# Half of each token row is gathered, the other half is brought to the experts by products with the slot matrix

## The chip, the cores and the metric

The kernel runs on one core of one Trainium2 chip. The metric is the device time of one execution in microseconds. All data is 32-bit floating point. The core has a matrix engine (TensorE, "PE" in the profile, its weight loads "PEld"), a vector engine (DVE), a scalar engine (ACT), GpSimd (POOL), a queue engine for transfers (SyncE, "SP") and 16 DMA engines that all transfers share. PE reads two operands from the on-chip memory (a stationary one, loaded first, and a moving one) and writes into eight banks of accumulators, from which ACT and DVE copy results out.

## What is computed

The reference is one step of a hybrid encoder layer for 384 tokens (256 of a prompt, 128 of eight samples) with 1024 features. The change is in its last part, the mixture of experts:

```
def _moe(h, p):
    scores = jax.nn.sigmoid((h @ p['router_w']).astype(jnp.float32))
    ...
    gates = jnp.einsum('blk,blke->ble', wsel, one_hot(eidx, N_EXPERTS))
    act = silu(einsum('ld,edf->lef', hs, we_gate)) * einsum('ld,edf->lef', hs, we_up)
    y = einsum('lef,efd->ld', act * gs[..., None], we_down)
    return y + (jax.nn.silu(h @ p['ws_gate']) * (h @ p['ws_up'])) @ p['ws_down']
```

The line left out is the group-limited choice of 8 of 64 experts for each token. Each expert has gate and up weights of 1024 x 256 and down weights of 256 x 1024, so 3 MB per expert. 384 tokens with 8 experts each make 3072 rows for the experts, 48 per expert on average.

## The kernel before, in words

Before the experts, the layer's projections, the two recurrent branches, the merge and the first normalisation run once over all tokens. Then the shared expert runs, and each token's input row (`h2_tok`, three tiles of 128 tokens x 1024 in token order) is stored to a DRAM table `h_rows` (L707, from ACT's queue).

The routed experts are done in 33 **tasks**. A task n below 32 is a pair of experts, 64 slots each, which fill the 128 columns; task 32 takes up to four overflow tiles of 32 slots. For a task:

- DVE's `spread(n)` makes the **slot matrix** `onehot`: for each of the three token tiles a 128 x 128 matrix of zeros and ones that says which token sits in which slot (L978).
- PE's `find(n)` (12 small matmuls, L2074) multiplies it with the token numbers, DVE's `ids(n)` writes the row number and the gate of each slot.
- POOL's `gather(n)` (L463) fetches the rows of 4 KB from `h_rows` with an indirect DMA, three tasks ahead, into one of three buffers `xt`.
- PE's `turn_in(n)` (L2063) turns the gathered 128 x 1024 tile by eight 128 x 128 transposes into banks 0 and 1. ACT's and DVE's `turned(n)` copy the two banks to `hgT`.
- PE multiplies `hgT` with the gate and up weights (L2108, 32 instructions; the two experts' columns run beside each other), ACT and DVE make the gated activation, PE turns it (L2115), `down(n)` multiplies it with the down weights (L2089, 16 instructions), ACT and DVE copy the result to `obuf`, and POOL's `scatter(n)` (L472) writes the rows of 4 KB to a DRAM table `y_rows`.

A 32-bit matmul is two instructions in the profile, a 32-bit transpose one. PE's order in its loop over n is written by hand: `turn_in(n + 1)`, the wait for the gate and up weights of task n, the gate and up matmuls of n, `down(n - 1)`, the transposes of the activation of n, `find(n + 3)`.

SP loads the weights (L528). There are four slots, two tasks' worth. SP waits until the gate and up matmuls of task n-2 are done and issues the four transfers for task n, then waits until `down(n-2)` is done and issues the two down transfers for task n. The wait on `down` holds back what follows it in the queue, so that at each end of a `down` six transfers of 1 MB are issued together: the down weights of one task and the gate and up weights of the next. After the last task the eight parts of each token are read back from `y_rows` and added.

`more(...)` holds the same steps for inputs with more than four overflow tiles. In this profile the gather of the tasks (L463) ran 33 times and the one in `more` not at all.

Of the kernel before, what the change touches and what calls it, by code (L numbers as in the profile page):

```python
# [4 lines left out]
F32 = mybir.dt.float32  # L5
# [53 lines left out]
def hybrid_kernel(nc, x_prompt, x_sample, c_prompt, c_sample, state_gdn_conv, state_gdn,  # L59
# [6 lines left out]
    with ctx:  # L66
# [91 lines left out]
        h_rows = nc.dram_tensor("h_rows", [T, D], F32).ap()  # L158
# [53 lines left out]
        h2_tok = [flat(zs, D), flat(gate, D), flat(lnx, D)]  # L212
        xt = flat(hT, 3 * D).rearrange("p (a n) -> p a n", a=3)
# [5 lines left out]
        onehot = flat(qkv, 2 * TILES * P, 4096).rearrange("p (a t c) -> p a t c", a=2, t=TILES)  # L219
        count = flat(lvl, NE)  # L220
# [139 lines left out]
        def _(pool):  # L360
# [90 lines left out]
            pool.wait_ge(S("h_out"), 32 + 16)  # L451
# [6 lines left out]
            def gather(n):  # L458
                pool.wait_ge(S("r_ids"), n + 1)
                if n >= 3:  # L460
                    pool.wait_ge(S("r_turn"), n - 2)
                mark()
                pool.indirect_dma_start(xt[:, n % 3, :], None, h_rows,  # L463
                                        bass.IndirectOffsetOnAxis(slot_ids[:, n % IDS, 0:1], 0),
                                        bounds_check=T - 1, oob_is_err=False
                                        ).then_inc(S(f"r_xg{n % 3}"), 16)
# [20 lines left out]
            def more(n_task):  # L487
                def gather(i, u):
                    pool.wait_ge(S("r_ids"), i * ROUND + u + 1 + past("ids"))
                    if not (isinstance(i, int) and i * ROUND + u < 2):  # L490
                        pool.wait_ge(S("r_turn"), i * ROUND + u - 1 + past("turn"))
                    mark()
                    pool.indirect_dma_start(xt[:, u % 2, :], None, h_rows,
                                            bass.IndirectOffsetOnAxis(slot_ids[:, u % ROUND, 0:1], 0),
                                            bounds_check=T - 1, oob_is_err=False
                                            ).then_inc(S(f"r_xg{u % 2}"), 16)
# [206 lines left out]
        def _(act):  # L703
# [188 lines left out]
            for t in range(3):  # L892
                load(h_rows[tok(t), :], h2_tok[t], "h_out")
# [28 lines left out]
            act.wait_ge(S("h_out"), 48)  # L922
# [50 lines left out]
        def _(dve):  # L973
# [445 lines left out]
            def spread(n):  # L1419

                hot = onehot[:, n % 2]
# [116 lines left out]
        def _(pe):  # L1538
# [518 lines left out]
            def turn_in(n):  # L2057
# [4 lines left out]
                for k in range(KC):  # L2062
                    last = tr(bank[k // 4][:, tok(k % 4)], xt[:, n % 3, tok(k)], ident[:, :])  # L2063
                sig(last, "r_turn")

            def find(n):
# [4 lines left out]
                for j, (cols, e) in enumerate(tiles_of(n)):  # L2071
                    for t in range(TILES):
                        rows = slot_rows[:, t, e, :] if n < N_PAIR else o_rows[:, t, j, :]
                        last = mm(bank[6][cols, 0:3], onehot[:, n % 2, t, cols], rows,  # L2074
# [48 lines left out]
            def more(n_task):  # L2123
                def turn_in(i, u):
                    pe.wait_ge(S(f"r_xg{u % 2}"), i * 48 + 16 * (u // 2 + 1) + past(f"xg{u % 2}"))
# [3 lines left out]
                    for k in range(KC):  # L2129
                        last = tr(bank[k // 4][:, tok(k % 4)], xt[:, u % 2, tok(k)], ident[:, :])  # L2130
# [101 lines left out]
```

## Time and profile before

| | us |
|---|---|
| median of 3 runs (1621.63 to 1632.64) | 1628.92 |
| the profiled execution, its own time | 1629.57 |
| its span, first to last instruction | 1627.8 |

| engine | busy us | share of the span |
|---|---|---|
| PE | 1298.6 | 80% |
| PEld | 755.5 | 46% |
| DVE | 525.2 | 32% |
| ACT | 239.8 | 15% |
| POOL | 161.2 | 10% |

A line of the page gives the line number of the kernel, the engine, the operation, the names written and read, and how often. In the chain of waits each piece has its start, its length and what it was; "issue" there is time in which the engine waited for nothing that the profile shows (a wait for several transfers is one such). "x32" counts instructions.

### The profile page before, as it was taken

The numbers are of one execution on the slowest core, as the hardware profiler recorded it, in microseconds if no ns is written. First come the engines' busy times: TensorE is split into PE (matmuls) and PEld (weight loads), VectorE is DVE, ScalarE is ACT, GpSimd is POOL, SyncE is SP. The second block draws the span as 40 slices with busy tenths as digits, with TensorE's granted clock in tenths as the row PEclk, the third lists the DMA queues.
The fourth block names the chain that finished last, engine by engine and source line by source line (L and its number), as shares of the span: only waits on it lengthen the run. The fifth ranks groups of instructions, "written<-read, shape, count | busy, mean of one in ns | idle before, by whom it ended". The sixth has DMA issues, their size and how long they took to land.

```text
span 1627.8 us, 15451 instructions
## 1 busy us (share of the span) xinstructions
PE 1298.6 (80%) x6250; PEld 755.5 (46%) x6250; DVE 525.2 (32%) x1085; ACT 239.8 (15%) x450; POOL 161.2 (10%) x196
## 2 busy tenths in 40 slices
PE   3789999687756998899799787878878878887446
PEld 1445555486634975796444543333333333333112
DVE  0432567445483233423325521311111111111007
ACT  2021441310010121121100211110110110110000
POOL 5000000030001400320000001010010010011000
PEclk8898899787877898999989789989888898989768
DMA  9365410300104001000550539999999999999655
GB/s 317 119 230 210 155 52 1 82 2 1 52 8 122 1 27 52 27 1 1 211 180 35 237 111 368 420 400 407 412 410 398 408 408 394 405 389 396 265 220 193
DMA packets 96504, 330.63 MB, mean 203 GB/s; under 512 B 20046, under 2 KB 37026, under 8 KB 69547
## 3 DMA queue, kind: packets, MB, share of 16 engines
q1 hardware_dynamic: 84230, 301.60, 48.0%
q0 software_dynamic: 9504, 25.18, 4.0%
q10 hardware_dynamic: 2692, 2.79, 0.6%
q8 instruction: 52, 0.85, 0.2%
q14 instruction: 26, 0.21, 0.0%
HBM read 314.75 MB, written 24.22 MB: 208 GB/s over the span
## 4 chain that ended last, share of the span: by engine, by line
PE 70%; DMA 10%; DVE 8%; issue 7%; SPq 3%; ACT 2%; POOL 0%; ACTq 0%; POOLq 0%; DVEq 0%
PE bank L2108 15%; PE bank L1610 9%; PE bank L2089 6%; DMA ring<-in_we_up_dram 6%; PE bank L1733 5%; PE bank L1794 3%; PE bank L1983 3%; PE bank L1951 3%; PE bank L1807 3%; PE bank L1804 2%; PE bank L2202 2%; SPq L528 2%; DVE inv L978 2%; DVE ring L978 2%; PE bank L2063 2%
## 5 line engine op out<-in xcount | busy, mean ns | idle before, releaser
L2108 PE MATMUL bank<-ring,rwp 128*64 128x512 f32 (+1 forms) x816 | 280.9, 693 | 123.8 <-issue 123.8
L2108 PEld LDWEIGHTS bank<-ring,rwp 128*64 128x64 f32 (+1 forms) x816 | 87.8, 157 | 289.2 <-issue 289.2
L1610 PE MATMUL bank<-hT,ring 128*128 128x384 f32 x416 | 145.4, 514 | 7.7 <-DVE hT L978 5.6
L2108 PE MATMUL bank<-MT,rwp 128*64 128x512 f32 (+1 forms) x272 | 144.7, 694 | 0.0
L987 DVE SCALAR_TENSOR_TENSOR seq_cols<-seq_cols,slot_gate,bank 128x256 f32<-128x256 f32 x33 | 22.1, 671 | 371.6 <-ACT seq_cols L710 371.6
L2089 PE MATMUL bank<-inv,rwp 128*64 128x512 f32 (+1 forms) x408 | 121.9, 615 | 8.8 <-DMA inv<-in_we_down_dram 8.8
L1610 PEld LDWEIGHTS bank<-hT,ring 128*128 128x128 f32 x416 | 83.3, 202 | 67.3 <-issue 9.8
L463 POOL DMA_INDIRECT hT<-h_rows,slot_ids x33 | 33.6, 1018 | 698.3 <-PE bank L2063 449.0
L1733 PE MATMUL bank<-hT,ring 128*128 128x384 f32 x256 | 89.6, 510 | 10.3 <-DMA ring<-in_w_in_dram 10.3
L710 ACT ACTIVATE seq_cols<-bank 128x256 f32<-128x256 f32 x36 | 13.8, 383 | 400.5 <-PE bank L2108 385.4
L1733 PEld LDWEIGHTS bank<-hT,ring 128*128 128x128 f32 x256 | 50.5, 201 | 44.2 <-DMA ring<-in_w_in_dram 10.4
L710 ACT ACTIVATE rwp<-bank 128x512 f32<-128x512 f32 (+1 forms) x101 | 43.5, 445 | 162.6 <-PE bank L1610 96.2
L978 DVE TENSOR_TENSOR inv<-inv,bank 128x256 f32<-128x256 f32 (+1 forms) x86 | 33.8, 428 | 96.2 <-PE bank L1807 90.5
L2089 PE MATMUL bank<-qkv,rwp 128*64 128x512 f32 (+1 forms) x136 | 64.0, 615 | 0.0
L2089 PEld LDWEIGHTS bank<-inv,rwp 128*64 128x64 f32 (+1 forms) x408 | 39.7, 139 | 47.0 <-issue 47.0
L1794 PE MATMUL bank<-inv 128*128 128x128 f32 x360 | 50.5, 301 | 6.2 <-POOL inv L446 6.2
L446 POOL TENSOR_TENSOR inv<-NT,lvl 128x512 f32<-128x512 f32 x18 | 22.8, 1267 | 327.7 <-DVE aT L978 280.3
L710 ACT ACTIVATE inv<-bank 128x512 f32<-128x512 f32 (+3 forms) x53 | 29.8, 571 | 147.4 <-PE bank L1794 129.6
L1794 PEld LDWEIGHTS bank<-inv 128*128 128x128 f32 x360 | 46.9, 211 | 8.1 <-POOL inv L446 8.1
L1807 PE MATMUL bank<-inv 128*128 128x64 f32 x360 | 49.0, 284 | 0.0
L446 POOL TENSOR_TENSOR inv<-MT,lvl 128x512 f32<-128x512 f32 x36 | 45.1, 1268 | 20.9 <-DVE MT L978 16.7
L1807 PEld LDWEIGHTS bank<-inv 128*128 128x128 f32 x360 | 45.9, 202 | 0.0
(362 smaller groups left out, 1799.1 us busy)
## 6 DMA issues: line engine op xcount, KB each, us to landing
ring<-in_we_gate_dram SPq DMA_DIRECT2D x51, 1024.0 KB, 13.4
ring<-in_we_up_dram SPq DMA_DIRECT2D x51, 1024.0 KB, 16.6
inv<-in_we_down_dram SPq DMA_DIRECT2D x51, 1024.0 KB, 10.9
ring<-in_w_ada_dram SPq DMA_DIRECT2D x12, 2048.0 KB, 14.2
MT<-in_we_gate_dram SPq DMA_DIRECT2D x17, 1024.0 KB, 16.7
MT<-in_we_up_dram SPq DMA_DIRECT2D x17, 1024.0 KB, 19.7
qkv<-in_we_down_dram SPq DMA_DIRECT2D x17, 1024.0 KB, 8.4
ring<-in_w_in_dram SPq DMA_DIRECT2D x7, 2048.0 KB, 9.1
```

The lines of the kernel that those rows point to most:

```text
L446: st.do(pool.tensor_tensor(NL[:, g].rearrange("p (h i) -> p h i", h=4), src, lvl[:, l, :].unsqueeze(1).broadcast_to([P, 4, P]), ALU.mult), ...
L463: pool.indirect_dma_start(xt[:, n % 3, :], None, h_rows, bass.IndirectOffsetOnAxis(slot_ids[:, n % IDS, 0:1], 0), bounds_check=T - 1, oob_ ...
L710: st.do(act.activation(out, in_, func, **kw), name, hold)
L978: st.do(V.tensor_tensor(out, a, b, op), name, hold)
L1610: last = mm(bank[4 + n % 4][:, 0:T], ring[:, u, k, tok(c)], hT[:, k, :], start=(k == 0), stop=(k == KC - 1))
L1733: last = mm(bank[bk][:, 0:T], mg_w[i % 3][:, k, tok(b % 2)], hT[:, k, :], start=(k == 0), stop=(k == KC - 1))
L1794: last = mm(bank[g][:, tok(h)], NL[:, g][:, tok(h)], X[:, g][:, tok(h)], start=True, stop=True)
L1807: last = mm(bank[g][:, 64 * h:64 * h + 64], T1[:, g][:, tok(h)], level_half(XT[:, g][:, tok(h)], l, 1), start=True, stop=True)
L1951: last = mm(bank[bk][:, 0:T], pab[w][:, k, tok(c)], yT[:, w, k, :], start=(k == 0), stop=(k == 3))
L1983: last = mm(bank[[4, 5, 6, 7, 0, 1][2 * t + i]][:, :], merged[:, k, tok(t)], w_o_sb[i][:, k, :], start=(k == 0), stop=(k == KC - 1))
L2089: last = mm(bank[4 + j][cols, :], actT[:, n % 2, tok(k)][:, cols], wd_slot[d_slot(e)][:, k, 512 * j:512 * j + 512], start=(k == 0), stop=( ...
L2108: last = mm(gu[cols, :], hgT[:, n % 2, k, cols], gate_up(gu_slot[w_slot(e)], k), start=(k == 0), stop=(k == KC - 1))
```

## The change

Every token row is split into two halves of 512. `h_rows` becomes two tables, each with one half, written by six stores and not three. The gather of a task fetches only the first half of each row (2 KB). The second half of the three `h2_tok` tiles stays on chip, and `turn_in` makes the turned second half by products: for each of four blocks of 128 features, the three token tiles' blocks as stationary operands times the three parts of the slot matrix, summed in bank 1. So `turn_in` has four transposes and twelve 128 x 128 x 128 products where it had eight transposes. As the slot matrix is now read later, it has three buffers (`hots`), the third in the place of `modT`. The path `more` gathers both halves with two DMAs.

```diff
--- before.py
+++ after.py
@@ -155,7 +155,7 @@
         over_e = ctx.enter_context(nc.sbuf_tensor("over_e", [P, N_OVER + 1], I32))
         tok_id = sb("tok_id", [P, TILES, 2])
 
-        h_rows = nc.dram_tensor("h_rows", [T, D], F32).ap()
+        h_rows = [nc.dram_tensor(f"h_rows{i}", [T, 512], F32).ap() for i in range(2)]
         y_rows = nc.dram_tensor("y_rows", [T * N_ACT, D], F32).ap()
 
 
@@ -209,14 +209,16 @@
         gu_slot = [flat(ring, 4096, 4096 * i) for i in range(3)] + [flat(MT, 4096)]
         wd_slot = [flat(t, 2048, off).rearrange("p (k n) -> p k n", k=2)
                    for t, off in ((inv, 0), (inv, 2048), (inv, 4096), (qkv, 0))]
-        h2_tok = [flat(zs, D), flat(gate, D), flat(lnx, D)]
-        xt = flat(hT, 3 * D).rearrange("p (a n) -> p a n", a=3)
+        h2_tok = [flat(zs, D, 512), flat(gate, D, 512), flat(lnx, D)]
+        xt = flat(hT, 3 * 512).rearrange("p (a n) -> p a n", a=3)
+        more_xt = flat(hT, 2 * D).rearrange("p (a n) -> p a n", a=2)
         hgT = flat(rwp, 2 * D, 2 * D).rearrange("p (a k c) -> p a k c", a=2, k=KC)
         obuf = [flat(zs, D), flat(gate, D)]
         sil = flat(seq_cols, 2 * DE).rearrange("p (a n) -> p a n", a=2)
         act_t = flat(seq_cols, 2 * DE, 2 * DE).rearrange("p (a n) -> p a n", a=2)
         actT = flat(rwp, 2 * DE, 4672).rearrange("p (a n) -> p a n", a=2)
         onehot = flat(qkv, 2 * TILES * P, 4096).rearrange("p (a t c) -> p a t c", a=2, t=TILES)
+        hots = [onehot[:, 0], onehot[:, 1], flat(modT, TILES * P).rearrange("p (t c) -> p t c", t=TILES)]
         count = flat(lvl, NE)
         n_over = flat(lvl, NE, NE)
         n_cum = flat(lvl, NE, 2 * NE)
@@ -448,7 +450,7 @@
                                                  ALU.mult), "inv_nl", hold=False)
 
 
-            pool.wait_ge(S("h_out"), 32 + 16)
+            pool.wait_ge(S("h_out"), 96)
             pool.wait_ge(S("sgu_mm"), 3)
 
             def mark():
@@ -460,7 +462,7 @@
                 if n >= 3:
                     pool.wait_ge(S("r_turn"), n - 2)
                 mark()
-                pool.indirect_dma_start(xt[:, n % 3, :], None, h_rows,
+                pool.indirect_dma_start(xt[:, n % 3, :], None, h_rows[0],
                                         bass.IndirectOffsetOnAxis(slot_ids[:, n % IDS, 0:1], 0),
                                         bounds_check=T - 1, oob_is_err=False
                                         ).then_inc(S(f"r_xg{n % 3}"), 16)
@@ -490,10 +492,11 @@
                     if not (isinstance(i, int) and i * ROUND + u < 2):
                         pool.wait_ge(S("r_turn"), i * ROUND + u - 1 + past("turn"))
                     mark()
-                    pool.indirect_dma_start(xt[:, u % 2, :], None, h_rows,
-                                            bass.IndirectOffsetOnAxis(slot_ids[:, u % ROUND, 0:1], 0),
-                                            bounds_check=T - 1, oob_is_err=False
-                                            ).then_inc(S(f"r_xg{u % 2}"), 16)
+                    for j in range(2):
+                        pool.indirect_dma_start(more_xt[:, u % 2, 512 * j:512 * j + 512], None, h_rows[j],
+                                                bass.IndirectOffsetOnAxis(slot_ids[:, u % ROUND, 0:1], 0),
+                                                bounds_check=T - 1, oob_is_err=False
+                                                ).then_inc(S(f"r_xg{u % 2}"), 16)
 
                 def scatter(i, u):
                     pool.wait_ge(S("r_oA"), i * ROUND + u + 1 + past("oA"))
@@ -890,7 +893,8 @@
                   bank[i][:, :].rearrange("p (m k) -> p m k", k=KC), ACT.Copy, "h2_tok", hold=False)
             act.wait_ge(S("h2_tok"), 6)
             for t in range(3):
-                load(h_rows[tok(t), :], h2_tok[t], "h_out")
+                for j in range(2):
+                    load(h_rows[j][tok(t), :], h2_tok[t][:, 512 * j:512 * j + 512], "h_out")
 
             for j in range(3):
                 act.wait_ge(S("sgu_mm"), j + 1)
@@ -919,7 +923,7 @@
                     act.wait_ge(S(f"r_sc{n % 2}"), 16 * (n // 2))
                 f(obuf[n % 2][:, 0:512], bank[4][:, :], ACT.Copy, "r_oA", hold=False)
 
-            act.wait_ge(S("h_out"), 48)
+            act.wait_ge(S("h_out"), 96)
             turned(0)
             for n in range(N_TASK):
                 if n + 1 < N_TASK:
@@ -1418,7 +1422,7 @@
 
             def spread(n):
 
-                hot = onehot[:, n % 2]
+                hot = hots[n % 3]
                 if n < N_PAIR:
                     tt(hot.rearrange("p t (a c) -> p t a c", a=2),
                        count_up[:, 0:HALF].unsqueeze(1).unsqueeze(1).broadcast_to([P, TILES, 2, HALF]),
@@ -2059,8 +2063,12 @@
                 if n:
                     pe.wait_ge(S("r_hgA"), n)
                     pe.wait_ge(S("r_hgD"), n)
-                for k in range(KC):
-                    last = tr(bank[k // 4][:, tok(k % 4)], xt[:, n % 3, tok(k)], ident[:, :])
+                for k in range(4):
+                    tr(bank[0][:, tok(k)], xt[:, n % 3, tok(k)], ident[:, :])
+                for k in range(4):
+                    for t in range(TILES):
+                        last = mm(bank[1][:, tok(k)], h2_tok[t][:, 512:D][:, tok(k)], hots[n % 3][:, t, :],
+                                  start=(t == 0), stop=(t == TILES - 1))
                 sig(last, "r_turn")
 
             def find(n):
@@ -2071,7 +2079,7 @@
                 for j, (cols, e) in enumerate(tiles_of(n)):
                     for t in range(TILES):
                         rows = slot_rows[:, t, e, :] if n < N_PAIR else o_rows[:, t, j, :]
-                        last = mm(bank[6][cols, 0:3], onehot[:, n % 2, t, cols], rows,
+                        last = mm(bank[6][cols, 0:3], hots[n % 3][:, t, cols], rows,
                                   start=(t == 0), stop=(t == TILES - 1))
                 sig(last, "r_ids_mm")
 
@@ -2122,12 +2130,12 @@
 
             def more(n_task):
                 def turn_in(i, u):
-                    pe.wait_ge(S(f"r_xg{u % 2}"), i * 48 + 16 * (u // 2 + 1) + past(f"xg{u % 2}"))
+                    pe.wait_ge(S(f"r_xg{u % 2}"), i * 96 + 32 * (u // 2 + 1) + past(f"xg{u % 2}"))
                     if not (isinstance(i, int) and i * ROUND + u < 1):
                         pe.wait_ge(S("r_hgA"), i * ROUND + u + past("hgA"))
                         pe.wait_ge(S("r_hgD"), i * ROUND + u + past("hgD"))
                     for k in range(KC):
-                        last = tr(bank[k // 4][:, tok(k % 4)], xt[:, u % 2, tok(k)], ident[:, :])
+                        last = tr(bank[k // 4][:, tok(k % 4)], more_xt[:, u % 2, tok(k)], ident[:, :])
                     last.then_inc(S("r_turn"), 1)
 
                 def find(i, u):
```

## Rows read from the trace of the kernel before

**Rows 1.** Page, span in 40 slices: PE clock in tenths, DMA engines' busy tenths.
```profile
PEclk8898899787877898999989789989888898989768
DMA  9365410300104001000550539999999999999655
```

**Rows 2.** Windows view, 985 to 1530 us: busy us, clock, DMA share, GB/s.
```profile
985.00:1530.00 545.00, 425.11 (x2128) 176.47 (x2124) 89.27 (x209) 56.80 (x123) 60.68 (x60) 0.88 0.99 403
```

**Rows 3.** DMA view, 985 to 1530 us: queue packets, MB, share of 16 engines; issues.
```profile
q1 hardware_dynamic: 26932, 196.13, 88.0%
q0 software_dynamic: 8761, 23.28, 11.0%
hT<-h_rows,slot_ids POOLq DMA_INDIRECT x29, 9.1
y_rows<-zs,slot_ids POOLq DMA_INDIRECT x16, 11.0
y_rows<-gate,slot_ids POOLq DMA_INDIRECT x15, 11.4
```

**Rows 4.** Chain of waits, one task of the stretch: start us, us, what.
```profile
1290.09 8.78 PE bank L2108 x32
1298.87 3.43 PE bank L2089 x16
1302.31 0.37 PE bank L2115 x2
1302.67 0.58 PE bank L2074 x12
1303.26 1.02 PE bank L2063 x8
1304.28 3.41 issue
1307.69 8.79 PE bank L2108 x32
```

**Rows 5.** Waits of PE, 985 to 1530 us: in total, times, longest us.
```profile
PE bank L2108 <- issue: 102.0, 29, 7.1
```

**Rows 6.** DMA view, 1096 to 1098 us, when only weights move.
```profile
DMA packets 106, 0.84 MB, mean 418 GB/s; under 512 B 4, under 2 KB 4, under 8 KB 4
```

**Rows 7.** DMA view, 60 to 100 us: loads whose rows are 2 KB.
```profile
q1 hardware_dynamic: 3106, 6.27, 43.4%
```

**Rows 8.** Timelines: one 32-bit product group L1794 at low clock, and later in the chain.
```profile
342.78 5.99 PE L1794 MATMUL bank<-inv 128*128 128x128 f32 x24 [1.30 <-POOL inv L446]
682.36 2.73 PE bank L1794 x24
```

**Rows 9.** Chain of waits, head of the expert stage.
```profile
959.73 4.48 DMA hT<-h_rows,slot_ids
964.25 1.98 PE bank L2063 x8
967.09 1.94 PE bank L2063 x8
969.03 7.71 PE bank L2108 x32
979.94 7.02 PE bank L2108 x32
```

**Rows 10.** Windows view at low clock: head of the stage, and inside one task.
```profile
964.00:967.00 3.00, 1.97 (x8) 1.57 (x8) 0.69 (x1) 0.60 (x1) 0.00 (x0) 0.50 0.71 262
1308.00:1312.00 4.00, 4.00 (x13) 1.39 (x11) 0.00 (x0) 0.00 (x0) 0.00 (x0) 0.57 1.03 394
```

**Rows 11.** Chain of waits, the last scatter, to its landing.
```profile
1563.25 2.97 DMA y_rows<-zs,slot_ids
```

**Rows 12.** Timeline of ACT's queue and the transpose that next needs ACT.
```profile
923.87 0.80 ACTq L707 DMA_DIRECT2D h_rows<-lnx  x1
933.66 0.14 PEld L2019 LDWEIGHTS bank<-ident,seq_cols 128*128 128x128 f32 x1 [0.24 <-issue]
```

## The prediction

> **What bounds the kernel now.** I read the slices of the page first [rows 1]. From about 980 to 1530 us the DMA engines stand at 9 or more, and the clock of PE sits between 8 and 9. That is the stage of the routed experts, the only one that the change touches. The windows view of 985 to 1530 us says it in one line [rows 2]: DMA share 0.99 at 403 GB/s, PE busy 425 of 545 us. The DMA view of the same stretch splits the engines' time [rows 3]: 88.0% for the queue with the weights (196.13 MB) and 11.0% for POOL's queue, which carries the rows of gathers and scatters (23.28 MB).
>
> The chain of waits shows one task [rows 4]. PE works 8.78 (gate and up), 3.43 (down), 0.37, 0.58 (find) and 1.02 us (`turn_in`), in all 14.18 us, and then stands 3.41 us. The next gate and up matmuls begin 17.60 us after the last ones. What PE waits for there is the last of the six weight transfers, which were issued at the end of an earlier `down`. The waits view gives the sum over the stretch: 102.0 us in 29 waits, 3.52 us each [rows 5]. So a task takes as long as its bytes need, and PE has 3.5 us to spare. The reader should also see that PE pays for this wait: the clock after it is at 0.57, so partly at the lower level of 1.2 GHz [rows 10], and a gate and up group takes 8.78 us where it took 7.02 at the full 2.4 GHz [rows 4, 9].
>
> **Part 1, the gather moves half.** In the stretch lie 29 gathers and 16 + 15 scatters [rows 3]. Both move the same rows of 4 KB, so the gathers' part is 29/60 of 23.28 MB, 11.25 MB, and 5.63 MB of that go. The price of a megabyte can be had in three ways. By the mean rate of 403 GB/s it is 2.48 us, and 5.63 MB are 14.0 us. By the queue's own share, 11.0% of 545 us for 23.28 MB, it is 2.58 us; but what is left moves in rows of 2 KB. Loads with such rows took 43.4% of 40 us for 6.27 MB, 2.77 us each MB [rows 7]. Then the gathers go from 11.25 x 2.58 = 29.0 to 5.63 x 2.77 = 15.6 us, a saving of 13.4. The upper end comes from what is left when weights alone move: 418 GB/s [rows 6] makes 469.2 us for 196.13 MB, the other 75.8 us of the stretch are 3.26 us for each MB of rows, and the saving would be 18.3. I take 14.0, which is nearest to the queue's own share, and keep 13.4 and 18.3. Per task it is 14.0/29 = 0.48 us, so 17.12 and not 17.60 us.
>
> **Part 2, the products.** `turn_in` loses four of eight transposes (0.51 of 1.02 us [rows 4]) and gains twelve products of 128 x 128 x 128, 24 instructions. The same form stands in the trace as a group of 24 at line 1794: 2.73 us at full clock, 5.99 us in a stretch at the low one [rows 8]. These are the two ends. In the stretch I take 2.73: `turn_in` then lasts 3.24 us, 2.22 more. PE's path is 14.18 + 2.22 = 16.40 us, under 17.12 by 0.72, even if gate and up stay at 8.78. With PE almost without a gap I expect the clock to stay up, gate and up at 7.02, and the path at 14.64. So the products cost nothing here; what hides them is the wait for weights. Without that cover they would cost 2.22 x 29 = 64 us.
>
> The weights' issue does not move away: SP issues at the end of a `down`, which comes 12.2 us or less after the weights of its task landed, so the transfers of the next task still stand in the queue for about 5 us. The engines do not run dry.
>
> **Part 3, the head of the stage.** Before the weights queue up there is nothing to hide behind. From the first gather on, the chain goes through `turn_in(0)`, `turn_in(1)`, gate and up (0), `turn_in(2)`, gate and up (1) and `down(0)` [rows 9]; only at the end of that does SP issue the first full batch, and from there on the DMA engines are the bound. A delay here passes to the end. The clock is at 0.50 from 964 to 967 us [rows 10]. Step by step:
> - The gather of half rows lands sooner. It took 4.48 us; the last scatter, with few rows, took 2.97 [rows 9, 11]. Between -1.5 and 0; I take -0.4, as most of the time is not the bytes'.
> - `turn_in(0)`, 1.98 us at low clock, becomes four transposes (0.99) and 24 instructions in 2.73 to 5.99. I take half of them at either clock: 5.36, so +3.4 (+1.7 to +5.0).
> - `turn_in(1)`, 1.94, becomes 3.24 at full clock: +1.3 (to +5.0, were it at low clock).
> - Gate and up (0) took 7.71 with its begin at low clock; at full clock it is 7.02 [rows 9]: -0.7 (or 0).
> - `turn_in(2)`: +2.2.
>
> Sum +5.8, from +3.0 to +12.2.
>
> From 964 to 967 us eight transposes kept PE busy 1.97 of 3.00 us, and the clock stayed at the low level [rows 10]. The Trainium skill, in "TensorE: Matmul & The Clock Gate", Part 4 (PE-mode transpose), says that a transpose doesn't count as a busy PE for the clock. By that rule the products, unlike the transposes, bring the clock up within the head, and the sum would be near the 5.8 above. If two thirds of busy time were simply too little, the head would stay at the low clock and the sum would be 12.2. This row agrees with the rule but doesn't prove it.
>
> **Edits at nothing.** ACT issues six stores and not three, at up to 0.80 us each [rows 12]; ACT's next result is wanted by the transposes that start at 933.66, some 9 us later, so up to 2.4 us are covered (2.4 if not). The stores land long before the first gather at 959.73 [rows 9], so POOL's and ACT's higher wait counts cost nothing. A gather stays one issue on POOL. It waits for `turn_in` of three tasks before, which is done a whole task before the `find` that it also needs, so a longer `turn_in` doesn't hold it, nor the scatter queued behind it. The copies of `turned` start up to 2.2 us later; behind them on ACT and DVE stand the activation of the task and `spread`, which are wanted only when gate and up end, some 8 us on. The third slot-matrix buffer adds no wait. The two-DMA gather of `more` doesn't run here.
>
> **Sum.** -14.0 + 5.8 = -8.2 us. The profiled execution took 1629.57 us, 0.65 above the median of 1628.92 and 1.77 above its span; against it the forecast is 1621.4, against the median 1620.7, so 1621. With the ends of the parts it runs from -18.3 + 3.0 = -15.3 to -13.4 + 12.2 = -1.2, 1613.6 to 1627.7.
>
> **Rivals.**
> - *The bytes buy no time.* If an engine pays for a row and not for its bytes, the 29 gathers cost what they did and only the head is left: +5.8, 1634.7 (1632 to 1641). Against it: 2 KB rows in a full stretch moved at 2.77 us per MB, close to the 2.58 of 4 KB rows [rows 3, 7]; for it: none of those is an indirect transfer. The Trainium skill, in "DMA: Bandwidth & Descriptors", Rules for kernel authors, advises to coalesce many small transfers into one large, which speaks for this rival; no row here shows an indirect transfer of 2 KB rows.
> - *PE becomes the bound, and the kernel slower.* The place is `turn_in` between a `down` and the next gate and up. The path without `turn_in` is 13.16 us with gate and up at 8.78, so it decides from a `turn_in` of 17.12 - 13.16 = 3.96 us (5.72 with gate and up at 7.02). With `turn_in` at the low clock, 0.99 + 5.99 = 6.98, the task takes 20.14 us, 2.54 more than now, 74 us over 29 tasks and with the head 1628.92 + 74 + 5.8 = 1709. With half of it low (5.36) it takes 18.52, 0.92 more, and 1661. For it: the margin of 0.72 us is small. Against it: the row of 682 us ran 24 such instructions in 2.73, and the low clock came after idle time that would then be gone.
> - *Rows cost more than their bytes, and the head is almost free.* The ends -18.3 and +3.0 together, or a little beyond: 1613 down to 1609. For it: the rate falls from 418 to 403 GB/s when rows mix in [rows 2, 6]. Against it: the queue's own share gives 2.58 us per MB, not 3.26.
>
> **How the numbers follow.** I give the forecast 0.68, no gain from the bytes 0.13, PE as the bound 0.11, the larger gain 0.08. The range reaches from the larger gain to the first rival, 1612 to 1637, and leaves out PE as the bound and the far ends of the others. A measurement of this kernel can tell about 1%, 16 us. Faster by more than that needs the larger gain beyond its ends: 0.09. Slower needs PE as the bound: 0.12. Within 1% the rest, 0.79.
>
> **What would show it.** In the profile after, POOL's queue should carry near 17.7 MB in the stretch, the DMA share should stay near 0.99 and the step from one gate and up to the next be near 17.1 us; the wait before it should shrink from 3.5 to between 0.7 and 2.5 us, and the clock there rise. The 24 product instructions should take near 2.73 us. The end of `down(0)`, now at 979.94 + 7.02 + 3.43 = 990.4 us [rows 4, 9], should come near 996. I am wrong if the DMA share falls below 0.95 or the wait before gate and up vanishes (PE is the bound), or if the step stays at 17.6 with half the bytes gathered.

## The result and the profile after

The changed kernel took 1609.61 us (median of 4 runs, 1607.46 to 1613.73), the kernel before 1630.78 in the same comparison: ratio 0.9884 [0.9841, 0.9928]. A second comparison on another chip gave 0.9893 [0.9868, 0.9919]. That is 17 to 19 us less, where 8.2 were forecast. The profiled execution took 1609.27 us, with a span of 1607.5.

The page after: the slices, in tenths as in [rows 1], and the line of POOL's queue (packets, MB, share). The clock of PE in the expert stage goes from 8 and 9 to 9 throughout.

```profile
PEclk7898899787877798899999799999999999999778
DMA  9365410300104001000532635999999999999655
...
q0 software_dynamic: 7392, 18.89, 3.1%
```

The windows view, with the columns of [rows 2, 10]: first the stage, which now ends near 1520, then 400 us of its middle, then two pieces of the head.

```profile
985.00:1520.00 535.00, 465.26 (x2774) 244.26 (x2774) 89.13 (x209) 56.80 (x123) 61.09 (x60) 0.96 0.98 402
1060.00:1460.00 400.00, 359.76 (x2139) 191.25 (x2138) 64.92 (x141) 43.56 (x94) 48.95 (x48) 0.98 1.00 411
964.00:967.00 3.00, 2.99 (x20) 2.80 (x19) 0.00 (x0) 0.00 (x0) 0.00 (x0) 0.74 0.03 14
967.00:970.00 3.00, 2.13 (x19) 2.17 (x20) 0.69 (x1) 0.60 (x1) 0.00 (x0) 1.00 0.00 0
```

DMA share and rate of the stage are about those of before, 0.98 and 402 GB/s for 0.99 and 403. What is new is PE: 465 of 535 us busy and a clock of 0.96, where it was 425 of 545 and 0.88. The DMA view of the same window answers to [rows 3].

```profile
q1 hardware_dynamic: 27061, 197.04, 89.3%
q0 software_dynamic: 6864, 17.75, 8.5%
hT<-h_rows,slot_ids POOLq DMA_INDIRECT x29, 7.2
```

POOL's queue carries 17.75 MB and not 23.28, as the change intends. The chain of waits, first through the head, then through one task, answers to [rows 9, 4]; L2070 are the products.

```profile
958.36 3.57 DMA hT<-h_rows,slot_ids
...
961.98 1.11 PE bank L2067 x4
963.09 3.92 PE bank L2070 x24
...
967.87 0.63 PE bank L2067 x4
968.50 2.68 PE bank L2070 x24
971.18 7.04 PE bank L2116 x32
...
980.39 0.59 PE bank L2067 x4
980.98 2.68 PE bank L2070 x24
983.66 7.02 PE bank L2116 x32
990.68 3.43 PE bank L2097 x16
...
1031.31 7.09 PE bank L2116 x32
1038.39 3.43 PE bank L2097 x16
1041.83 0.37 PE bank L2123 x2
1042.19 0.58 PE bank L2082 x12
1042.78 0.59 PE bank L2067 x4
1043.37 2.68 PE bank L2070 x24
1046.05 1.53 issue
1047.58 7.09 PE bank L2116 x32
```

A task takes 16.27 us here (1031.31 to 1047.58): gate and up 7.09 and not 8.78, and 1.53 us of waiting. The waits view of PE, 985 to 1515 us, says the same of the stretch, where [rows 5] had 102.0 us.

```profile
PE bank L2116 <- issue: 48.2, 28, 3.3
```

So the bytes, the products, the clock and the wait came as forecast, and still the kernel gained twice as much: the step from one gate and up to the next is 16.8 us on average over 24 tasks, where 17.1 were forecast. I split the stage at one point, the end of `down(0)`, from which on the DMA engines set the time. From the first gather to there the chain takes 30.7 us before (959.73 to 990.4) and 35.8 after: the head lost 5.1 us, near the forecast. From there to the begin of the last gate and up group, called the **stretch** below, it is 543.5 us before and 521.7 after: 21.9 us less, where 14.0 were forecast. The question is where the other 8 us are from.

### The profile page after: what moved, and what is told of

Same layout as the page of the kernel before. It is cut to its first block, busy times and chain, and to the rows that moved or that the text cites. A ratio compares the mean times of both kernels' runs of the same rounds, so it can differ in the third digit from the quotient of the medians.

```text
span 1607.5 us, 16774 instructions
## 1 busy us (share of the span) xinstructions
PE 1336.0 (83%) x6910; PEld 828.0 (52%) x6910; DVE 524.9 (33%) x1085; ACT 239.8 (15%) x450; POOL 161.7 (10%) x196
## 3 DMA queue, kind: packets, MB, share of 16 engines
q1 hardware_dynamic: 84230, 301.60, 48.2%
q0 software_dynamic: 7392, 18.89, 3.1%
## 4 chain that ended last, share of the span: by engine, by line
PE 78%; DVE 8%; DMA 5%; issue 4%; SPq 2%; ACT 2%; POOL 0%; ACTq 0%; POOLq 0%; DVEq 0%
PE bank L2116 15%; PE bank L1614 9%; PE bank L2097 7%; PE bank L2070 6%; PE bank L1737 5%; PE bank L1798 3%; PE bank L1987 3%; PE bank L1955 3%; PE bank L1811 3%; PE bank L1808 2%; DVE inv L982 2%; PE bank L2210 2%; DVE ring L982 2%; SPq L531 2%; DMA ring<-in_w_in_dram 1%
## 5 line engine op out<-in xcount | busy, mean ns | idle before, releaser
L2116 PE MATMUL bank<-ring,rwp 128*64 128x512 f32 (+1 forms) x816 | 244.9, 618 | 69.7 <-issue 69.7
L2116 PEld LDWEIGHTS bank<-ring,rwp 128*64 128x64 f32 (+1 forms) x816 | 80.5, 140 | 203.4 <-issue 202.9
L2116 PE MATMUL bank<-MT,rwp 128*64 128x512 f32 (+1 forms) x272 | 128.5, 628 | 0.0
L994 DVE COPY rwp<-bank 128x512 f32<-128x512 f32 (+1 forms) x34 | 23.2, 682 | 101.6 <-PE bank L2070 101.0
L1798 PEld LDWEIGHTS bank<-inv 128*128 128x128 f32 x360 | 46.9, 211 | 8.1 <-POOL inv L448 8.1
L448 POOL TENSOR_TENSOR inv<-MT,lvl 128x512 f32<-128x512 f32 x36 | 45.2, 1267 | 20.9 <-DVE MT L982 16.7
## 6 DMA issues: line engine op xcount, KB each, us to landing
ring<-in_w_ada_dram SPq DMA_DIRECT2D x12, 2048.0 KB, 14.3
```

Of the source, the lines that this page charges most:

```text
L448: st.do(pool.tensor_tensor(NL[:, g].rearrange("p (h i) -> p h i", h=4), src, lvl[:, l, :].unsqueeze(1).broadcast_to([P, 4, P]), ALU.mult), ...
L1798: last = mm(bank[g][:, tok(h)], NL[:, g][:, tok(h)], X[:, g][:, tok(h)], start=True, stop=True)
L2116: last = mm(gu[cols, :], hgT[:, n % 2, k, cols], gate_up(gu_slot[w_slot(e)], k), start=(k == 0), stop=(k == KC - 1))
```

## The experiments

Times are ratios to the kernel before on the same chip, with 95% intervals; us are the ratio less 1, times 1629. Executions of the kernel before lie up to 16 us apart on one chip, so a single time decides nothing. The table has every run; "order" is an edit of SP's queue that comes with the third set. The stretch is read from one profiled execution of each kernel, so a difference of a few us between two stretches is not secured; the changed kernel, profiled twice, gave 521.7 and 522.9. The profiled execution was the slowest of its kernel for the half gather alone (3.7 us over the median), no gather (6.1) and the late issue (6.9).

| kernel | ratio | us | stretch us |
|---|---|---|---|
| before | 1 | 0 | 543.5 |
| changed kernel | 0.9884 [0.9841, 0.9928] | -18.9 | 521.7 |
| half gather alone | 0.9927 [0.9902, 0.9953] | -11.9 | 531.6 |
| products alone | 1.0024 [0.9996, 1.0052] | +3.9 | 539.5 |
| changed kernel, again | 0.9893 [0.9868, 0.9919] | -17.4 | 522.9 |
| no gather | 0.9833 [0.9775, 0.9892] | -27.2 | 517.3 |
| half scatter | 0.9886 [0.9857, 0.9915] | -18.6 | 525.6 |
| before + order | 0.9948 [0.9928, 0.9968] | -8.5 | 535.8 |
| half gather + order | 0.9813 [0.9788, 0.9839] | -30.5 | 516.7 |
| products + order | 0.9969 [0.9951, 0.9988] | -5.0 | 533.1 |
| changed + order | 0.9857 [0.9832, 0.9882] | -23.3 | 515.8 |
| changed + order, first three whole | 0.9840 [0.9815, 0.9864] | -26.1 | 517.5 |
| the same, quarter gather | 0.9777 [0.9753, 0.9800] | -36.3 | 507.5 |
| before, issue later | 1.0075 [1.0053, 1.0097] | +12.2 | 565.5 |

**Half the gather alone, the products alone.** Either part of the change by itself. In the first, `turn_in` makes eight transposes of the half that is there; in the second, the gather moves whole rows that are only half used.

```diff
-        h_rows = nc.dram_tensor("h_rows", [T, D], F32).ap()
+        h_rows = nc.dram_tensor("h_rows", [T, 512], F32).ap()
...
-                    last = tr(bank[k // 4][:, tok(k % 4)], xt[:, n % 3, tok(k)], ident[:, :])
+                    last = tr(bank[k // 4][:, tok(k % 4)], xt[:, n % 3, tok(k % 4)], ident[:, :])
```

> The kernel before with a gather of the first half of each row alone; turn_in makes eight transposes of that half, each block twice, so the second half of the experts' inputs is replaced by the first. No products. I compare the stretch from the end of down(0) to the begin of the gate and up group of task 32: 543.5 us before, 521.7 us in the changed kernel. Theory 'rows': a gathered megabyte costs the DMA engines 3.9 us, far more than its share of the mean rate, and nothing else matters; then the stretch is near 522 us here too, and as the head has no products the whole is about 5 to 6 us under the changed kernel, near 1604. Rival 'PE': the products fill PE's wait and keep its clock up, so a down ends sooner after its weights, SP issues sooner and the queue of weights is fuller; that gave the 8 us beyond the bytes. Then the stretch is near 529.5 and the whole near 1612.

```diff
-        h_rows = [nc.dram_tensor(f"h_rows{i}", [T, 512], F32).ap() for i in range(2)]
+        h_rows = nc.dram_tensor("h_rows", [T, D], F32).ap()
```

> The changed kernel with the whole rows gathered again (one table, 4 KB rows), while turn_in still makes the second half by the products. Theory 'rows': the stretch is back at 543.5 us, and the head is 5 to 6 us longer than before, so the whole is near 1636, slower than before. Rival 'PE': the products alone shorten the stretch by 8 us to 535.5, and the whole is near 1628.

The half gather alone gave 11.9 us, with an interval from 7.7 to 16.0 that holds the 14.0 of the forecast; in the stretch it is 11.9 too, much less than the 21.9 of the whole change. The products alone cost 3.9 us in all, with an interval that just reaches 0; their head is 5.6 us longer (36.25 us), and their stretch 4.0 us shorter. So the parts don't add up: 11.9 - 3.9 = 8.0, close to the forecast of 8.2, but together they gave 17.4, which is more by 9.4 us, with about 7 either way. Something in the products makes the half gather worth more.

**No gather, half scatter.** Two sizes of the same price, in the kernel before.

```diff
-                pool.indirect_dma_start(xt[:, n % 3, :], None, h_rows,
-                                        bass.IndirectOffsetOnAxis(slot_ids[:, n % IDS, 0:1], 0),
-                                        bounds_check=T - 1, oob_is_err=False
-                                        ).then_inc(S(f"r_xg{n % 3}"), 16)
```

> The kernel before without any gather: turn_in transposes what lies in the buffers, so the experts' inputs are left out. Theory 'rows' with a price that goes with the bytes: 11.25 MB at 3.9 us take 44 us out of the stretch, which is then near 499.5 us, and with a head 4 us shorter the whole is near 1583. If instead each gather has a fixed part that halving its bytes did not touch, more than twice 21.8 us go; if the first half saved is dearer than the second (the engines' idle time ends), less: by the mean rate the other half is worth 14 us, a stretch of 508 and a whole near 1591. The rival 'PE' gives 28 us from bytes, a stretch of 515.5 and a whole near 1599.

```diff
-        y_rows = nc.dram_tensor("y_rows", [T * N_ACT, D], F32).ap()
+        y_rows = nc.dram_tensor("y_rows", [T * N_ACT, 512], F32).ap()
```

> The kernel before with the scatter of the first half of each result row alone; the final sum reads that half twice, so the second half of the experts' results is replaced by the first, and the reads at the end move as many bytes in twice as many transfers. It prices the other kind of rows: 31 scatters with some 12.0 MB in the stretch, of which 6.0 MB go. If only gathered rows are dear, these cost the mean rate, 2.48 us per MB: 15 us, a stretch of 528.5. If rows on POOL's queue are dear in general, at 3.9 us per MB, 23 us and 520. What is left of the 74 us that all rows cost over weights alone after 44 for the gathers, 30 us, gives 15 for the half.

Without any gather the stretch falls by 26.2 us; the first half of the bytes gave 11.9 of them, so the second half is worth 14.3, no clear difference for one execution of each. Half of the scattered rows gave 17.9 in the stretch, so rows written are no cheaper than rows read. Halving the rows paid in both, so the first rival, that the bytes buy no time, falls.

**The changed kernel again**, for the comparisons of this set.

> The changed kernel once more, beside the next three and the same runs of the kernel before. Half gather alone gave a ratio of 0.9927 and products alone 1.0024; if the two parts add up, the changed kernel is near 0.995 (1615); if the products help the half gather in the stretch (a warm clock ends a down sooner, so the queue of weights never runs dry), it is near the 0.988 of its first comparison (1604 to 1610).

It gave the result once more: 0.9893.

**Gate and up weights issued first.** In the chain of the kernel before stands a passage that I had not read. The first line gives the shares of 1060 to 1460 us by line, the others one task and a half.

```profile
by line: PE bank L2108 45.1%; issue 18.2%; PE bank L2089 16.5%; DMA ring<-in_we_up_dram 11.5%; PE bank L2063 4.1%; PE bank L2074 2.3%; PE bank L2115 1.5%; SPq L528 0.9%
...
1080.37 10.07 PE bank L2108 x32
1090.43 3.45 PE bank L2089 x16
...
1093.90 0.33 SPq L528
...
1095.41 14.71 DMA ring<-in_we_up_dram
1110.12 5.39 issue
1115.52 9.56 PE bank L2108 x32
```

Here the end waits for a transfer that waits for its own issue, by SP (L528), at the end of a `down` that comes late: gate and up took 10.07 us at a clock of 0.70. The transfer named takes 14.71 us from its issue to its landing. It is the fourth of the six issued there; the 5.39 us behind it are the wait for the sixth, which by the trace's records lands at 1115.42, 21.5 us after the first issue. The six are 6.29 MB, which at the 418 GB/s of [rows 6] need 15.0 us by themselves, so the landings alone don't say whether the queue had run empty. The engines' share does: from 1094 to 1095 us it falls to 0.60. The chain passes so in five places of the stretch, at 1093.90, 1128.54, 1251.10, 1462.68 and 1511.78 us. The windows view of the kernel before shows the dip as the issue comes: 1.5 us around the end of two `down`s, and below them 1060 to 1460 us.

```profile
1285.60:1287.10 1.50, 1.50 (x19) 0.95 (x17) 0.77 (x3) 0.87 (x2) 0.00 (x0) 1.00 0.73 257
1301.80:1303.30 1.50, 1.50 (x19) 0.88 (x16) 0.70 (x2) 0.87 (x2) 0.00 (x0) 1.00 1.00 421
1060.00:1460.00 400.00, 321.43 (x1578) 133.00 (x1580) 61.52 (x135) 41.35 (x90) 46.32 (x46) 0.88 1.00 405
```

In the first the DMA share is 0.73, one task later 1.00. Over the 400 us it rounds to 1.00, as after, and only the rate, 405 for 411 GB/s, tells the two apart. In the chain of the changed kernel, 1060 to 1460 us, no transfer stands at all:

```profile
by line: PE bank L2116 44.6%; PE bank L2097 20.5%; PE bank L2070 16.0%; issue 10.1%; PE bank L2067 3.4%; PE bank L2082 3.4%; PE bank L2123 2.1%
```

That made a theory: the products keep PE busy while it waits, the clock stays up, `down` ends sooner, the six transfers are issued before the queue is empty, and only then half the rows are worth all their time. To test it without products I let SP issue the gate and up weights of the task after next as soon as their slots are free, ahead of the wait on `down` that held them back.

```diff
-            for n in range(2, N_PAIR):
-                sp_.wait_ge(S("r_gu_mm"), n - 1)
-                for e in (2 * n, 2 * n + 1):
-                    load_gu(e, e)
+            sp_.wait_ge(S("r_gu_mm"), 1)
+            for e in (4, 5):
+                load_gu(e, e)
+            for n in range(2, N_PAIR):
+                if n + 1 < N_PAIR:
+                    sp_.wait_ge(S("r_gu_mm"), n)
+                    for e in (2 * n + 2, 2 * n + 3):
+                        load_gu(e, e)
                 sp_.wait_ge(S("r_dn_mm"), n - 1)
```

> The kernel before with one edit in SP's order: the four gate and up transfers of a task are issued when the gate and up matmuls two tasks before are done, ahead of the wait on down and of the two down transfers, so some 3.4 us earlier. Bytes and PE's work are the same. Theory 'queue': in the kernel before, the DMA engines ran dry or thin for some 0.2 us per task, since new weights are issued only 5.4 us before the old ones have landed; with 8.8 us ahead that goes, 4 to 8 us in the stretch, and 3.4 us more as the first full batch starts sooner: ratio near 0.995. Rival: the queue was full anyway and all of the extra gain is rows; then only the 3.4 us of the begin are left or nothing, a ratio of 0.998 to 1.0.

> The changed kernel with the same edit in SP's order. Theory 'queue': here the products have already filled the queue (new weights come 5.9 us ahead, the engines' idle share is nil), so only the earlier begin is left: 3 to 4 us under the changed kernel. If the edit gives as much as in the kernel before plus its 4 to 8 us, the products had not filled the queue.

The kernel before gained 8.5 us by this order alone, with the same bytes and the same clock (0.871 and 0.869 over the span). In the middle 400 us the engines now move 414 GB/s, where it was 405:

```profile
1060.00:1460.00 400.00, 323.16 (x1617) 135.60 (x1614) 63.13 (x138) 42.59 (x92) 46.60 (x46) 0.89 1.01 414
```

So its queue had room to be filled. It isn't quite full with the order either: transfers hold 9.8% of the chain in these 400 us, where they held 11.5%. The changed kernel gained 5.9 more, with about 6 either way, so whether the order gives it less than the kernel before isn't settled.

**Half gather with the order, products with the order.** The same edit on the two part kernels. If the order does what the products did, the half gather should gain as much without them.

> The half gather alone (no products, eight transposes of the first half, so the second half of the experts' inputs is replaced by the first) with SP's edit (gate and up transfers issued ahead of the wait on down). Theory 'queue': the products help the stretch only by keeping the queue of weights filled; SP's edit fills it as well, so this kernel has all that the changed kernel with SP's edit has, less the products in the head (5.1 us): ratio near 0.983. Rival: the products help in another way; then the half gather (0.9927) and SP's edit (0.9948) only add up, 0.9875 or above.

> Whole rows gathered, products in turn_in, and SP's edit. Theory 'queue': with the queue filled by SP's edit the products have nothing left to give and cost only the head, 5.6 us: SP's edit alone gave 0.9948, so 0.998. Rival (the products help by themselves, 4 us and more in the stretch): 0.995 or less.

The half gather with the order gave 0.9813, where its 11.9 and the 8.5 of the order add up to 0.9875. (In its profiled execution the stage began at 952.75, some 6 us sooner than in the others, for no reason that I know; the stretch holds nothing of that.) In its chain from 1060 to 1460 us no transfer is left, as in the changed kernel, and its clock there is only 0.91; in the chain of the half gather alone the transfers had 14.9%.

```profile
by line: PE bank L2112 50.7%; PE bank L2093 20.6%; issue 17.7%; PE bank L2067 6.1%; PE bank L2078 3.3%; PE bank L2119 2.2%
...
1060.00:1460.00 400.00, 332.06 (x1680) 142.43 (x1680) 65.25 (x142) 44.49 (x97) 49.46 (x49) 0.91 1.01 417
```

```profile
by line: PE bank L2108 42.1%; issue 18.1%; PE bank L2089 16.3%; DMA ring<-in_we_up_dram 14.9%; PE bank L2063 3.8%; PE bank L2074 2.2%; PE bank L2115 1.4%; SPq L528 1.3%
```

So the worth of the half gather in the stretch is 11.9 us alone (543.5 - 531.6), 17.9 with the products (539.5 - 521.7, or 16.7 by the second run), 19.2 with the order (535.8 - 516.7) and 17.3 with both. By the ratios it is 11.9, 21.3, 22.0 and 18.3, each with 4 to 6 us either way, so that the first lies clearly below the second and the third, and not clearly below the fourth. Whatever fills the queue, products or order, lifts it. The other side of the table: the products cost 3.9 us alone and 7.2 with half gather and order, but bring 5.5 with the half gather. Once the order fills the queue, products bring the half gather nothing and cost their head. The products with the order, at 0.9969, lie between the two theories and nearer to the queue's; the interval holds its 0.998 and ends at 0.9951, just short of the other's 0.995.

**The kernel before, issued later.** The opposite edit: SP also waits for `turn_in`, so the six transfers are issued some 2 us later.

```diff
+                sp_.wait_ge(S("r_turn"), n + 2)
                 sp_.wait_ge(S("r_dn_mm"), n - 1)
```

> The kernel before with the cost in question doubled: SP waits, besides down, for the transposes of turn_in that follow it, so the six transfers are issued some 2 us later and only 3.4 us before the last weights in the queue have landed. Theory 'queue': the engines run dry for longer, 0.3 to 1.0 us more in each of 29 tasks: 9 to 29 us slower, ratio 1.005 to 1.018. Rival (the queue is deep enough and the issue's time does not matter): 1.000, or 1.001 for the later begin.

It cost 12.2 us (the profiled execution is its slowest, 1649.61 for a median of 1642.71, so the stretch in the table shows more). The DMA view from 1060 to 1460 us: the two queues sum to 96.3% of the engines; in the same window of the kernel before, the second fence, to 99.6%.

```profile
q1 hardware_dynamic: 18916, 137.75, 85.0%
q0 software_dynamic: 6336, 17.13, 11.3%
...
1060.00:1460.00 400.00, 308.05 (x1531) 128.38 (x1529) 59.89 (x132) 40.35 (x87) 44.57 (x44) 0.87 0.97 388
```

```profile
q1 hardware_dynamic: 19744, 143.79, 88.1%
q0 software_dynamic: 6624, 17.80, 11.5%
```

Averaged over 1060 to 1460 us from the trace's transfer records, in bins of 0.5 us around the issue of the down weights, the busy share of the engines dips to 0.62 here, 0.83 before, 0.84 with the half gather alone, 0.88 with the products alone, 0.92 in the changed kernel and in the kernel before with the order, and 0.96 with half gather and order. So the DMA share before was not full, and half the rows alone don't mend that.

The same records split each stretch into the time of the rows' packets, the time of the weights' packets (both in us of all 16 engines) and the rest, which is idle time of the engines and some 1 us of other queues; it falls below zero where the times of packets overlap. The rest is given up to the last 40 us of the stretch, and for these.

| kernel | stretch us | rows | weights | rest | rest of the last 40 us |
|---|---|---|---|---|---|
| before | 543.5 | 59.3 | 477.4 | 3.5 | 3.4 |
| half gather alone | 531.6 | 46.3 | 476.6 | 6.2 | 2.5 |
| products alone | 539.5 | 58.6 | 475.5 | 1.8 | 3.6 |
| changed kernel | 521.7 | 45.1 | 472.9 | 0.7 | 3.0 |
| before + order | 535.8 | 58.2 | 470.4 | 0.2 | 7.1 |
| half gather + order | 516.7 | 44.9 | 468.1 | -3.0 | 6.7 |
| before, issue later | 565.5 | 60.6 | 481.1 | 22.2 | 1.6 |

Of the 21.9 us of the changed kernel, 14.2 are the rows' packets, 4.5 the packets of the same weights (195 MB), and 3.2 the rest. The half gather alone takes 13.0 off the rows' packets, but the engines stand idle 1.9 us longer: fewer rows in the queue empty it sooner. The late issue pays 16.9 of its 21.9 us in the rest. The order takes 7.0 off the weights' packets, of which some 0.9 are bytes that moved before the stretch, and 3.3 off the rest, and pays 3.6 back in the last 40 us. The dip shows in the packets too: a weights' packet of 8 KB takes 309 ns at the median in all of these runs, but one that starts between 1 and 2 us after the issue takes 368 on average in the kernel before, 339 in the changed one.

**The first three tasks whole**, to give back the head: with the order, tasks 0 to 2 are gathered with both halves and turned by transposes.

```diff
+                    if n < 3:
+                        last = tr(bank[1][:, tok(k)], xt2[:, n % 3, tok(k)], ident[:, :])
+                        continue
                     for t in range(TILES):
                         last = mm(bank[1][:, tok(k)], h2_tok
```

> The changed kernel with the edit in SP's order, and with the first three tasks gathered whole (a second DMA for the other half, and eight transposes), so that the head of the stage has no products. The head was 5.1 us longer in the changed kernel from the first gather to the end of down(0); if the products there are the cause, these 5 us come back, less about 1 us for the second gather's issue: 4 us under the kernel with the SP edit alone, some 7 to 8 us under the changed kernel, near 1602.

The head fell from 35.7 to 32.6 us, and the kernel to 0.9840, 2.8 us below the changed kernel with the order: the right sign and about the size of the 3.1 us, though the intervals overlap.

**A quarter gathered.** As the queue is now filled and PE still waits a little, the last step moves another quarter of the row from the gather to the products: 36 product instructions a task, and 1 KB of each row gathered.

```diff
+        h_rows = [nc.dram_tensor(f"h_rows{i}", [T, (256, 768)[i]], F32).ap() for i in range(2)]
...
-                for k in range(4):
+                for k in range(2):
                     tr(bank[0][:, tok(k)], xt[:, n % 3, tok(k)], ident[:, :])
```

> A candidate for a better version: the kernel with SP's edit and the first three tasks gathered whole (0.984), and from the fourth task on a gather of a quarter row (1 KB) and products for the other six blocks of features, 36 product instructions. The rows' own time falls by another 0.25 us per task, 7 us: 0.980, if PE keeps up: its path is 7.1 + 3.43 + 0.95 + 0.26 + 36 x 0.112 = 15.8 us with gate and up at full clock, against some 16.3 for the bytes. If the clock falls in the gaps (8.8), PE has 17.5 and is the bound: then as slow as the changed kernel or slower, 0.99.

This is the best version: 0.9777 [0.9753, 0.9800], 1594.4 us, better than both kernels. Its chain shows a task without any wait, 15.80 us long (1219.91 to 1235.71), and its window both resources at their end: PE busy 394 of 400 us at full clock, DMA share 1.01.

```profile
1219.91 7.02 PE bank L2126 x32
1226.93 3.43 PE bank L2107 x16
1230.36 0.37 PE bank L2133 x2
1230.73 0.58 PE bank L2092 x12
1231.32 0.37 PE bank L2074 x2
1231.69 4.02 PE bank L2080 x36
1235.71 7.02 PE bank L2126 x32
...
1060.00:1460.00 400.00, 394.34 (x2495) 216.99 (x2494) 67.88 (x147) 46.33 (x100) 50.19 (x50) 1.00 1.01 420
```

## Why the prediction was wrong

- **What bounds the kernel: half right.** The DMA engines do set the time, but "DMA share 0.99" was read as a queue that is always full. It was an average over tasks with dips, and the chain that I read in one undisturbed task [rows 4] passed in five others through SP's issue.
- **Part 1, the gather's bytes: right, and so was their price.** 5.5 MB left the queue (23.28 to 17.75). The packets of the rows take 14.2 us less of all 16 engines in the stretch, where 14.0 were forecast; without any gather it is some 29 less, which is what Part 1 had for whole rows. With the queue filled the half gather was worth 17.3 to 19.2 in the stretch, about the upper end of 18.3, but its rows' packets fell by no more than 13.3 to 13.5 there; the others came off the weights' packets and the idle time. So that end came near as a number, and not as the price of a row's bytes that it was worked out as.
- **Part 2, the products hidden in the wait: right as far as it goes.** 2.68 us for 24 instructions (forecast 2.73), gate and up down to 7.02 to 7.09 in the tasks shown, a wait of 1.7 us each (48.2 in 28; forecast 0.7 to 2.5).
- **The step that failed** is the sentence behind it: "The engines do not run dry." From it followed that an earlier end of `down` is worth nothing, so that a faster gate and up was counted at zero in the stretch. From 1060 to 1460 us the mean gate and up group went from 8.77 to 7.44 us, and the mean lead of the issue ahead of the next gate and up from 5.4 to 5.9. What the runs showed in its place: around the issue the engines' share dips to 0.83, and of the 21.9 us of the stretch 7.7 are idle time and weights' packets, which the forecast had at nothing. The late-issue run shows that this lead has a price of its own, 12.2 us lost for some 2 us; the order gained 8.5, but it also puts gate and up ahead of `down` in the queue, and no run took the two apart. The "about 5 us" were reckoned to the landing of the last transfer, and the engines do not all have work to its end: ahead of task 32 no weights stand behind that transfer, and there the share is 0.26 over its last 2.5 us (1530.5 to 1533.0).
- **Sum.** The stretch is 21.9 us shorter: 4.0 by the products alone, 17.9 by the half gather on top of them. The head takes 5.1. That leaves 16.8, beside 17.4 and 18.9 measured; the forecast had 14.0, 0 and 5.8.
- **Part 3, the head: right.** The chain has `turn_in(0)` at 5.03 us (forecast 5.36, was 1.98), `turn_in(1)` 3.31 (3.24), gate and up (0) 7.04 (7.02), `turn_in(2)` 3.27 (3.24), the gather's landing 0.9 sooner (0.4). The sum is +5.1 for +5.8, and `down(0)` ends at 994.1 (forecast near 996, but the stage also began 1.4 us sooner).
- **The clock of the head.** After it stands at 0.74 from 964 to 967 us and at 1.00 in the next three, where eight transposes had left it at 0.50 [rows 10]. The rule on transposes that was weighed there, of the Trainium skill's "TensorE: Matmul & The Clock Gate", Part 4 (PE-mode transpose), agrees with that, and its smaller sum was the one that came. The run doesn't separate it from the other reading given there: with the products PE is also busier, 2.99 of the first 3.00 us where it was 1.97.
- **The rivals.** That the bytes buy no time falls with every run that halves them; as the packets were halved with them, which of the two is paid for stays open. PE didn't become the bound: it still waited 1.53 us in the task shown. Nearest in size was the larger gain, held at 0.08, but not in its cause: the head was not free, and the rest came off idle time and the weights' packets.

**What stays open.** Why the half gather takes weights' packets and idle time off as well, once products or order have come, isn't settled: with either it is worth 17 to 19 us in the stretch, where its rows' packets take 13 to 14. One could think that the rows are spread unevenly over the 16 engines and that the slowest engine counts; the profile gives their mean alone, and no other order of the rows was tried. That the clock is how the products fill the queue is argued and not shown: the gate and up groups became shorter (7.66 us on average with the products alone, from 8.77), and the order edit did much the same without them, but no run held the clock down with the products in place.

## What to carry to other kernels

A DMA share of 0.99 doesn't say that the queue never runs empty: look at the share in half microseconds around the issue, and for places where the chain passes through the issuing queue. Where the share dips there, an earlier issue can be worth time, and so can work put into the matrix engine's wait; here that seems to act through the clock and an earlier end. Before adding work for that, look whether a wait in the issuing queue holds back transfers that need not wait for it: here that edit alone gave 8.5 us, with every byte still moved.

## What the runs showed of the hardware that was not expected

- POOL's queue has 9504 packets over the whole span before and 7392 after. The 33 gathers of 128 slots make 4224 of them, and half of these, 2112, are gone: by the transfer records two rows of 2 KB travel in one packet of 4096 bytes (1521 of them beside the 3072 of the scatters). Halving the row so halved the packets too.
- With a filled queue the shares of the queues sum to more than 100% of the engines (92.9 + 7.7 with the quarter gather): the times of packets overlap a little, and the share can't be read to the last per cent.
- Products of zeros and ones bring up the clock for the matmuls behind them: gate and up (0), which now follows two `turn_in`s with 48 product instructions, took 7.04 us for 7.71 [rows 9], with a granted clock of 1.00 from 967 to 970 us, where it was 0.50.
